# Mixture-of-experts weight streaming on one Trainium2 core: expert gathers moved into the narrow slots, and a ring of ten weight buffers in place of nine

## The reference

```
logits = h @ router_w                       # 256 x 8
top_val, top_idx = lax.top_k(logits, 2)
gates = softmax(top_val)
for e in range(8):                          # w1, w3: 1024 x 3584; w2: 3584 x 1024
    out = out + dense_gate[..., e:e+1] * ((silu(h @ w1[e]) * (h @ w3[e])) @ w2[e])
```

## Time and profile before

| | |
|---|---|
| median of 3 runs | 1826.64 us (1820.36 to 1828.71) |
| profiled execution | 1822.02 us, span 1820.1 us |
| PE / DVE / ACT busy | 93% / 47% / 41% of the span |
| DMA | 473.82 MB, mean 260 GB/s |
| expert weight loads | 223 + 76 + 37 = 336 of 1024.0 KB |
| first and last expert load issued | 878.2 us, 1785.1 us |

### The profile page before, as it was taken

How to read it: one execution, slowest core, us unless ns; L and a number is a source line. 1 busy time by engine, 2 the same in 40 slices (tenths; PEclk the granted TensorE clock), 3 DMA queues, 4 the chain that set the end, 5 groups by cost and what they waited for, 6 DMA issues and landing times.

```text
span 1820.1 us, 22016 instructions
## 1 busy us (share of the span) xinstructions
PE 1688.8 (93%) x9050; PEld 1205.1 (66%) x9050; DVE 850.9 (47%) x994; ACT 742.7 (41%) x919; POOL 26.0 (1%) x27
## 2 busy tenths in 40 slices
PE   6998898999999999989999996999979999799986
PEld 5887476888888867756778732787228862388622
DVE  4334735332323345255588600886018850188501
ACT  5332635222223235346467501674016740177301
POOL 0000000000000000130000000000000000000000
PEclk8999998999999998999899999999999999999999
DMA  9654043623322237062889899999999999999996
GB/s 336 195 178 139 29 134 116 208 93 101 108 93 93 93 113 240 0 200 90 290 299 368 327 409 399 393 394 374 411 397 394 393 370 410 396 394 394 370 409 262
DMA packets 238636, 473.82 MB, mean 260 GB/s; under 512 B 16120, under 2 KB 115376, under 8 KB 238528
## 3 DMA queue, kind: packets, MB, share of 16 engines
q1 hardware_dynamic: 238144, 471.38, 71.1%
q0 software_dynamic: 384, 0.95, 0.3%
HBM read 471.25 MB, written 1.05 MB: 259 GB/s over the span
## 4 chain that ended last, share of the span: by engine, by line
PE 77%; DMA 11%; DVE 5%; SPq 3%; ACT 3%; issue 1%; DVEq 0%; ACTq 0%
PE bank L641 20%; PE bank L643 19%; PE bank L642 19%; PE bank L2520 6%; DMA raw_weights<-in_moe_w 6%; SPq L1224 2%; DMA spare_weights<-in_moe_w 2%; PE bank L708 2%; DMA y<-in_moe_w 2%; PE bank L2537 1%; PE bank L2415 1%; PE bank L2453 1%; PE bank L498 1%; PE bank L716 1%; DMA raw_weights<-in_w_mod 1%
## 5 line engine op out<-in xcount | busy, mean ns | idle before, releaser
L641 PE MATMUL bank<-h_high,split_high 128*128 128x512 f32 (+1 forms) x832 | 317.8, 382 | 6.7 <-DVE h_low L555 4.0
L642 PE MATMUL bank<-h_low,split_high 128*128 128x512 f32 (+1 forms) x832 | 314.8, 378 | 0.0
L643 PE MATMUL bank<-h_high,split_low 128*128 128x512 f32 (+1 forms) x832 | 314.8, 378 | 0.0
L625 DVE TENSOR_TENSOR split_low<-raw_weights,split_high 128x1024 fp32r<-128x1024 f32 x118 | 144.0, 1225 | 292.7 <-ACT split_high L620 292.7
L620 ACT ACTIVATE split_high<-raw_weights 128x1024 fp32r<-128x1024 f32 x118 | 124.1, 1056 | 188.6 <-PE bank L643 183.9
L1848 DVE TENSOR_TENSOR split_low<-raw_weights,split_high 128x2048 fp32r<-128x2048 f32 x74 | 169.3, 2289 | 50.0 <-ACT split_high L1560 49.5
L641 PEld LDWEIGHTS bank<-h_high,split_high 128*128 128x128 f32 x832 | 159.0, 191 | 39.7 <-issue 7.8
L643 PEld LDWEIGHTS bank<-h_high,split_low 128*128 128x128 f32 x832 | 158.7, 191 | 28.9
L642 PEld LDWEIGHTS bank<-h_low,split_high 128*128 128x128 f32 x832 | 159.0, 191 | 28.0
L1560 ACT ACTIVATE split_high<-raw_weights 128x2048 fp32r<-128x2048 f32 x74 | 141.9, 1918 | 53.8 <-PE bank L643 51.9
L2520 PE MATMUL bank<-raw_weights,xe_narrow 128*64 128x512 f32 (+1 forms) x696 | 138.6, 539 | 16.9 <-DMA raw_weights<-in_moe_w 16.6
(11 more groups left out here) (315 smaller groups left out, 2530.0 us busy)
## 6 DMA issues: line engine op xcount, KB each, us to landing
raw_weights<-in_moe_w SPq DMA_DIRECT2D x223, 1024.0 KB, 14.0
spare_weights<-in_moe_w SPq DMA_DIRECT2D x76, 1024.0 KB, 13.9
raw_weights<-in_w_mod SPq DMA_DIRECT2D x48, 1024.0 KB, 6.3
y<-in_moe_w SPq DMA_DIRECT2D x37, 1024.0 KB, 13.9
raw_weights<-in_ffn_w SPq DMA_DIRECT2D x33, 1024.0 KB, 5.2
raw_weights<-in_ev_w_in SPq DMA_DIRECT2D x10, 1024.0 KB, 9.5
raw_weights<-in_od_w_in SPq DMA_DIRECT2D x8, 1024.0 KB, 6.7
raw_weights<-in_ev_w_out SPq DMA_DIRECT2D x4, 1024.0 KB, 6.5
```

The lines of the kernel that those rows point to most:

```text
L625: dve.tensor_tensor(half_of(s, j, SPL[:, s % NSPLIT, :]), half_of(s, j, raw_of(split_at[s])), half_of(s, j, SPH[:, s % NSPLIT, :]).bitcast ...
L641: pe.matmul(ps, wh, xh, start=first, stop=False)
L642: pe.matmul(ps, wh, xl, start=False, stop=False)
L643: return pe.matmul(ps, wl, xh, start=False, stop=last)
```

## The change

Four things are changed together.

1. **A tenth ring buffer.** A third spare buffer, at place 8 of the ring, ahead of y. Its room comes from two places: ye_high and ye_low become one fp32 tile `ye` (also used by narrow slots), and mod_row_buffers move into the overlay, under the new buffer, which is loaded once the last modulation row has been turned.
2. **Gathers inside narrow slots.** Slot 0 picks only the tokens of slot 1. Narrow slots 1, 3 and 5 pick those of e+1 and e+2: groups 0 and 1 after d0, groups 2 and 3 after d1, in banks 5 and 7 in turn (so groups 2 and 3 wait for xe_low of groups 0 and 1), and the transposed one-hots after d2. Slots 2, 4 and 6 pick nothing; their last `turn` moves between the two units of d5. xe_narrow gets a second buffer in a dead table.
3. **Whole fp32 combine of wide slots.** Four true fp32 matmuls from `ye` in place of eight rounded ones; DVE's ye_low is gone.
4. **Bookkeeping** of groups, one-hot buffers and semaphores that follows from these.

```diff
-NSPARE = 2
+NSPARE = 3
 NRING = NSPARE + NRAW + 1
+SPARES = (0, 1, NRING - 2)
...
-        YEN = under("ye_narrow", [P, 512])
-        YEH, YEL = sb("ye_high", [P, D], F32R), sb("ye_low", [P, D], F32R)
+        YE = sb("ye", [P, D])
...
-            return e + 1 < NE if b else e % 2 == 0
+            return e + 1 < NE if b else e == 0
+
+        def gathers_inside(b, e):
+
+            return narrow(b, e) and e + 2 < NE
...
-            if b or e < 0:
-                return (e + 1,)
-            return tuple(i for i in (e + 1, e + 2) if i < NE)
+            return (e + 1,) if b or e < 1 else (e + 1, e + 2)
...
+        def xbank(b, e, r):
+
+            return (5, 7)[r % 2] if e >= 0 and gathers_inside(b, e) else XBANK[r]
...
+                    elif b == 0 and n == SPARES[2]:
+                        sp.wait_ge(S("mod_turned"), 24)
...
+                            if p in (1, 2) and gathers_inside(b, e):
+                                xe_high(e, 2 * p - 2)
+                                xe_high(e, 2 * p - 1)
+                        if p == 3 and gathers_inside(b, e):
                                 onehot_turned(e)
...
+                            if p == 1 and gathers_inside(b, e):
+                                onehots(e, SPOS)
+                            if p in (1, 2) and gathers_inside(b, e):
+                                xe_low(e, 2 * p - 2)
+                                xe_low(e, 2 * p - 1)
...
+                    if r >= 2 and e >= 0 and gathers_inside(b, e):
+                        pe.wait_ge(S("xe_low"), tokens_of(b, e + 1)[1] + r - 1)
...
-                        pe.matmul(PS[CBANK[r]][:, :], turned, YEH[:, y], start=True, stop=False)
-                        pe.matmul(PS[CBANK[r]][:, :], turned, YEL[:, y], start=False, stop=True)\
+                        pe.matmul(PS[CBANK[r]][:, :], turned.bitcast(F32), YE[:, y], start=True, stop=True)\
                           .then_inc(S("comb_full"), 1)
...
                             narrow_down(e, i, p)
+                            if p < 2 and gathers_inside(b, e):
+                                dispatch(e, 2 * p)
+                                dispatch(e, 2 * p + 1)
+                            if p == 2 and gathers_inside(b, e):
+                                pe.wait_ge(S("xe_low"), tokens_of(b, e + 1)[1] + 4)
+                                turn_onehots(e)
```

More of the change, by code:

```diff
@@ L1232, in experts @@
                         sp.wait_ge(*raw_free(b, *units[n - NRING]))
-                    elif b == 0 and n < NSPARE:
+                    elif b == 0 and n < SPARES[1] + 1:
                         sp.wait_ge(S("y_evac1"), 1)
-                    elif b == 0 and n < NRING - 1:
-                        sem, v = release[len(UNITS) - NRAW + n - NSPARE]
+                    elif b == 0 and n < SPARES[2]:
+                        sem, v = release[len(UNITS) - NRAW + n - 2]
                         sp.wait_ge(S(sem), v)
+                    elif b == 0 and n == SPARES[2]:
+                        sp.wait_ge(S("mod_turned"), 24)
                     elif b == 0:
@@ L1515, in xe_high @@
                     act.wait_ge(S("xe_full"), 4 * group(b, e + 1) + r + 1)
-                    src = PS[XBANK[r]][:, :].rearrange("p (f e n) -> p f e n", f=2, e=2)
+                    src = PS[xbank(b, e, r)][:, :].rearrange("p (f e n) -> p f e n", f=2, e=2)
                     for i, s in enumerate(gathered(b, e)):
                         if narrow(b, s):
-                            last = act.activation(XEN[:, 2 * r:2 * r + 2, :], src[:, :, i, 0:NARROW], ACT.Copy)
+                            last = act.activation(XEN[s // 2 % 2][:, 2 * r:2 * r + 2, :], src[:, :, i, 0:NARROW], ACT.Copy)
                         else:
@@ L1571, in narrow_slot @@
                             gt_whole(e, p - 1)
-                        if p == 1:
+                        if e == 1 and p == 1:
+                            onehot_turned(0)
+                        if p in (1, 2) and gathers_inside(b, e):
+                            xe_high(e, 2 * p - 2)
+                            xe_high(e, 2 * p - 1)
+                        if p == 3 and gathers_inside(b, e):
                             onehot_turned(e)
@@ L2000, in gates @@
                     dve.tensor_copy(SM[:, 60:61].bitcast(I32), SM[:, 57:58]).then_inc(S("routed"), 1)
[L2002 to L2008, removed]
                 def gather(e):
@@ L2061, in experts @@
                         if i == 0:
-                            if e >= 1 and not narrow(b, e - 1):
-                                ye_low(e - 1)
                             continue
@@ L2082, in experts @@
                             xe_low(e, 3)
-                if not narrow(b, NE - 1):
-                    ye_low(NE - 1)
                 gather(NE - 1)
@@ L2396, in turn_onehots @@
                 def turn_onehots(e):
-                    for i in range(len(gathered(b, e - 1))):
+                    for i in range(len(gathered(b, e))):
                         for t in range(2):
@@ L2414, in dispatch @@
                                 k = P * (2 * r + f)
-                                last = pe.matmul(PS[XBANK[r]][:, 256 * f:256 * f + P * n_slots], half[:, t, k:k + P],
+                                last = pe.matmul(PS[xbank(b, e, r)][:, 256 * f:256 * f + P * n_slots], half[:, t, k:k + P],
                                                  MP[:, t, 0:n_slots, :], start=(n == 0), stop=(n == 3))
@@ L2492, in narrow_combine @@
                             pe.matmul(PS[CBANK[t + 2 * c]][:, :], turned[rows, P * t:P * t + P],
-                                      YEN[rows, :], start=True, stop=True).then_inc(S("comb_full"), 1)
+                                      YE[rows, 0:512], start=True, stop=True).then_inc(S("comb_full"), 1)
                 def combine_last(e):
@@ L2555, in narrow_slot @@
                             narrow_up(e, i, "b", p)
-                            if p == 1:
-                                turn_onehots(e)
+                            if e == 1 and p == 1:
+                                turn_onehots(0)
                         else:
```

50 lines of the change are left out of this document (25 added, 25 removed).

## The result

The changed kernel takes 1809.62 us (median of 5 runs, 1808.99 to 1813.72) against 1824.07 us for the kernel before (5 runs): ratio 0.9925, 95% interval 0.9908 to 0.9943. The profiled execution took 1809.34 us with a span of 1807.5 us, 12.6 us under the span before; -13.1 was forecast.

The account below looks back on a forecast made before the run. Loads were taken to bound the kernel from slot 1 on, PE slot 0. Terms -2.6 - 11.2 - 0.35 + 1.0 = -13.1 us, against a median of 1826.6, gave 1813.5 us, range 1805 to 1823.

Parts of the forecast that it names:

- The bound: From slot 1 on only bytes count, and time is lost only where DMA has nothing to do; slot 0 is PE-bound.
- Three dips: Load-rate dips after wide slots 2, 4 and 6, worth 12.7 us, should close with gathers moved and buffer added: -11.2 us.
- Either part alone would nearly do it: At ends of slots 2, 4, 6: 1.0 unit left without the gather, 0.5 with the tenth buffer alone.
- Tenth buffer after slot 0: At the end of PE-bound slot 0, one more unit has landed with ten buffers: -2.6 us.
- Gather in slot 0: Picking for one expert in place of two, its halves go from 1.91 to 1.74 us: -0.35 us.
- Gather in narrow slots: In slots 1, 3, 5, 3.83 us of PE hidden by 17 us of slack: cost 0; 11.5 us if uncovered.
- Last `turn`: In wide slots, moved ahead of DVE's product with 2.7 us of cover: cost 0, upper end 1 us a slot.
- Fp32 combine: After a0 of narrow slots, 3.8 us in place of 2.03; hidden in slots 3, 5, 7; slot 1 costs +1.0 us.
- The ceiling on the mean: Rival: memory allows some 392 GB/s over two slots, so closed dips are paid back: 1825 us, chance 0.05.
- Halved dips: Rival: the dips after slots 2, 4 and 6 stay by half: -7.6, 1819 us, chance 0.16.
- The clock: Rival: new waits drop PE's clock to 1.2 GHz inside narrow slots: +24, 1851 us, chance 0.05.
- The signs: Right if windows after slots 2, 4, 6 read 395 GB/s or more, pairs take about 220 us, SP's gap some 6 us.

Follow-up runs that it names:

- e5: The changed kernel with eight ring buffers in place of ten; ratio 1.0025 to the kernel before.
- e3: The changed kernel with nine buffers and the old two-part combine, gathers still inside narrow slots; ratio 0.9940 to the kernel before.
- e1: The kernel before plus the tenth buffer and the fp32 combine, gathers left in wide slots; ratio 0.9970 to the kernel before.
- e2: The changed kernel with nine buffers, the third spare left unused; ratio 0.9952 to the kernel before.
- e4: The kernel before with only the fp32 combine changed, nine buffers, gathers in wide slots; ratio 1.0015 to the kernel before.
- e6: The changed kernel with each gather group of slots 1, 3 and 5 made three times; ratio 0.9927 to the kernel before.
- e7: The changed kernel with each gather group of slots 1, 3 and 5 made seven times; ratio 1.0146 to the kernel before.
- e8: The changed kernel with the wide combine one item later, after b0 in place of a0; ratio 0.9915 to the kernel before.

## Why the prediction was right, point by point

- **The bound.** Right for narrow and wide slots taken together, by the table of rests and by e5: loads from slot 1 on, with time lost where the queue is dry or thin. "Only bytes count" says too much of a wide slot by itself, where PE never rests.
- **Two slips in the working.** The slices of the earlier trace rows up to the zero sum to 3.3 MB, not 6.6; the 3.15 units made from them are right. The count of 3.4 units is that of slot 2 alone; by the packets slots 4 and 6 end with 3.2 and 3.0.
- **Three dips (-11.2 us forecast).** The windows of the changed kernel give -3.7, -4.1 and -3.6 = -11.4 us. The mechanism is shown, but that the size came out so well is in part luck. Counted from the packets of the changed kernel, as loads issued less units moved, 4.0 units were outstanding at the last issue of slot 2 in place of 4.4, and the gap was 5.3 us in place of 6.2. The two misses cancel: 1.9 units were left when frees began again, where 2.0 were forecast. At the ends of slots 4 and 6 it was 1.7 and 1.3, and the window of the last is the one that still loses 0.8 us.
- **"Either part alone would nearly do it"** was wrong. The move alone leaves 3.1 us of 12.4 in slots 3, 5 and 7 (e3), the tenth buffer with the fp32 combine 9.8 us (e1). The step that failed is the count of outstanding units: I carried 3.4 + 1 = 4.4 units into a kernel with ten buffers, where 3.8 were there, and took a queue with half a unit in it for one that delivers 410 GB/s. Together the parts had room enough, so the sum did not suffer.
- **Tenth buffer after slot 0 (-2.6 us).** One unit fits every row of the second table, e5's with the other sign. It can be counted as well: when the combine after a0 of slot 1 stops the frees, the changed kernel and e1 have issued 56 loads, e2 and e4 55, e5 54.
- **Gather in slot 0 (-0.35 us).** Each half took 1.74 us in place of 1.91, as the earlier trace rows had let expect; its effect on the end is under the scatter ahead of slot 1.
- **Gather in narrow slots (0).** Right: three times the work costs nothing that can be measured (e6). Slack 9 us, where I had 17 - 5.6 = 11. A half took 2.10 us in place of 1.91.
- **Last `turn` (0).** From the landing of its first unit to a0 of slot 3, slot 2 takes 1257.78 - 1132.06 = 125.7 us, before 1262.19 - 1132.25 = 129.9 (the starts of the first copy, 0.02 us behind the landing): 4.2 us less for 3.83 us of matmuls. No wait appeared.
- **Fp32 combine (+1.0 us, 3.8 us each).** It takes 3.63 us; the loss of slot 1 rose by 1.1 us. That it is hidden in slots 3, 5 and 7 fits the queue there: 4.0 units ahead of the pause in slot 3 and 1.9 after it, where 3.3 and 1.1 were worked out.
- **The rivals.** The ceiling on the mean is refuted for this kernel: the windows at the changes went to 409 and 410 GB/s, and 394 in the wide slots and 409 in the narrow ones stayed. The Trainium skill's figure of 358 GB/s ("DMA: Bandwidth & Descriptors", "Where 436 GB/s comes from") does not bind here; this trace disagrees with it, as the one before did. Halved dips did not come; without the move of the gathers it would have been worse than that, with 9.8 of 12.4 us left in e1. The clock stayed at 1.00 in the narrow slots (1.00 over the 35 us windows, and over slots 3, 5 and 7 from a0 to their last load), and even e7, where PE never rests, is slower by its work alone.
- **The signs.** The three windows (409, 410, 401 GB/s), the pairs of slots, the last load and its 16 us behind, the combine's 3.63 us came as forecast. The window after slot 0 reads 238 GB/s where 215 to 235 stood, and the gap is 5.3 us where some 6 stood.
- **The medians.** The kernel before came out at 1824.07 in five runs where I had 1826.6, so the forecast of 1813.5 was 3.9 us high in time and 1.4 us short in difference.

## What to carry to other kernels

Where loads bound a stretch, look for the moments when nothing frees a buffer, count the loads outstanding at the last free from the rate curve, and compare with the length of the gap: work between two frees costs DMA time even on an engine with slack over the whole slot. Moving such work to where the queue is deep and adding a buffer both help, and here each left part of the dips that the two together closed: this queue needed nearly two 1 MiB loads outstanding at the worst moment. With 1.9 and 1.7 left the windows of the changed kernel read 409 GB/s, with 1.3 left 401, and with 0.5 or 0.6 left (e3) 397 to 399. A buffer is also worth one load, 2.6 us here, at the point where a compute-bound stretch hands over to a load-bound one.

## What the runs showed that I had not expected

**The start of slot 1 scatters by 6 us.** a0 of slot 1 begins between 1036.4 us (e7) and 1042.5 us (e1) in the ten profiled executions. Ahead of slot 1 the kernels differ only in where the modulation rows lie, in how many loads the ring takes and in 0.35 us of gather; the changed kernel, e6, e7 and e8 are the same program up to there and give 1038.7, 1041.6, 1036.4 and 1036.7 us. In windows of the kernel before and the changed one, PE is busy all of 893 to 896 us with small matmuls, and the granted clock falls from 1.00 to 0.50, earlier after the change (mean 0.59) than before (0.75). The second row is the changed kernel's:

```profile
893.00:896.00 3.00, 3.00 (x25) 3.00 (x24) 2.61 (x12) 3.00 (x6) 0.00 (x0) 0.75 1.06 389
```

```profile
893.00:896.00 3.00, 3.00 (x21) 3.00 (x19) 2.61 (x12) 3.00 (x6) 0.00 (x0) 0.59 1.06 388
```

The gather ahead of slot 0 then starts 0.9 us later (906.61 against 905.71 us). Over all kernels this gather starts between 904.0 us (e7) and 909.9 us (e1), so nearly the whole scatter is there before slot 0. Whether the clock makes all of it is open: from 885 to 895 us it was 1.00 in e1 and e6, the two that start latest, and 0.97 in the kernel before.

**A thin queue does not deliver the full rate.** In the earlier trace rows the five slices from 1263.5 us (33, 0, 0, 115 and 82 GB/s) make 2.2 us of the 3.8 us that the window of slot 3 loses before the change. The rest goes in thin slices before and after them, of 205 to 360 GB/s where loads are issued 1.3 to 2.0 us apart. In e3 the queue never runs dry after slots 2, 4 and 6, with 0.5 or 0.6 units left at the worst moment, and each window still loses about 1 us.

**ACT stands at the gather for long.** In the changed kernel ACT waits 102.5 us in sum for gather groups ahead of xe_high (16 waits), because its stream is written in that order. In narrow slot 3 it is busy 8.7 of 94.6 us, and from 1060 to 1257 us PE never waits for these copies.
